# The second feed-forward product of two layers, computed as seven block products instead of eight

## The reference, cut to what matters

```python
def swiglu(h, w_gu, w_down):
    gu = jnp.einsum('bsd,df->bsf', h, w_gu)
    g, up = gu[..., :D_FF], gu[..., D_FF:]          # D_FF = 2816
    return jnp.einsum('bsf,fd->bsd', jax.nn.silu(g) * up, w_down)

# second_block, in each of two layers:
h = layer_norm(ALPHA * h + mix, ln1_g[l], ln1_b[l])
h = layer_norm(ALPHA * h + swiglu(h, w_gu[l], w_down[l]), ln2_g[l], ln2_b[l])
```

## Time and profile before

| | before |
|---|---|
| median of 3 runs | 1973.95 us (1970.31 to 1974.38) |
| span of the profiled execution, first to last instruction | 1972.4 us |
| mean granted TensorE clock | 0.971 of full speed |
| TensorE matmuls busy | 1825.4 us, 93% of the span, 10396 matmuls |
| VectorE, ScalarE, GpSimd busy | 978.2, 760.7 and 407.5 us |
| down phase of layer 0 | 1244.8 to 1364.5 us |
| down phase of layer 1 | 1840.6 to 1960.3 us |

### The profile page before, as it was taken

The page is one execution under the profiler, slowest core; times in us unless marked ns, Lnnn a source line. Parts: engine busy times, 40 slices in busy tenths (PEclk is TensorE's granted clock), DMA queues, the critical chain, the costliest instruction groups (busy, mean ns, idle before and its releaser), DMA issues.

```text
span 1972.4 us, 26603 instructions
## 1 busy us (share of the span) xinstructions
PE 1825.4 (93%) x10396; PEld 1443.2 (73%) x10396; DVE 978.2 (50%) x1919; ACT 760.7 (39%) x1392; POOL 407.5 (21%) x450
## 2 busy tenths in 40 slices
PE   7999999996998764998999999999998999999997
PEld 6888777785554434776888888888776788888886
...
PEclk9999999996999996998999999999998999999999
DMA  4344300576999993221233333232211233332321
GB/s 161 86 114 129 97 2 2 168 294 235 382 387 402 392 346 119 74 65 44 87 96 106 97 96 97 97 98 81 76 60 48 76 106 98 100 100 88 106 97 53
DMA packets 134884, 264.42 MB, mean 134 GB/s; under 512 B 11617, under 2 KB 92129, under 8 KB 122465
## 3 DMA queue, kind: packets, MB, share of 16 engines
q1 hardware_dynamic: 116752, 229.92, 33.9%
...
q0 software_dynamic: 5120, 8.40, 1.3%
...
## 4 chain that ended last, share of the span: by engine, by line
PE 54%; DMA 10%; DVE 8%; issue 2%; ACT 1%; POOL 1%; PEld 1%; PEldq 0%; POOLq 0%; ACTq 0%; DVEq 0%; SPq 0%
PE b L507 15%; PE b L509 15%; PE b L508 15%; DMA m<-in_w_gate_up 6%; PE b L2054 3%; PE b L2607 2%; DMA m<-in_w_down 1%; DVE m L2782 1%; PE b L2079 1%; PE b L2589 1%; PE b L2575 1%; DMA m<-in_w_in 1%; DVE m L715 1%; DMA s_h<-m 1%; DVE m L657 1%
## 5 line engine op out<-in xcount | busy, mean ns | idle before, releaser
L507 PE MATMUL b<-m,m 128*128 128x512 f32 (+3 forms) x2060 | 777.2, 377 | 9.8 <-DVE m L2536 4.6
L508 PE MATMUL b<-m,m 128*128 128x512 f32 (+3 forms) x2060 | 768.9, 373 | 0.0
L509 PE MATMUL b<-m,m 128*128 128x512 f32 (+3 forms) x2060 | 768.6, 373 | 0.0
L493 DVE TENSOR_TENSOR m<-m,m 128x1024 fp32r<-128x1024 f32 (+1 forms) x212 | 278.6, 1320 | 480.3 <-ACT m L483 479.6
L507 PEld LDWEIGHTS b<-m,m 128*128 128x128 f32 x2060 | 390.2, 189 | 83.9 <-issue 6.0
L509 PEld LDWEIGHTS b<-m,m 128*128 128x128 f32 x2060 | 390.0, 189 | 66.2
L508 PEld LDWEIGHTS b<-m,m 128*128 128x128 f32 x2060 | 390.4, 189 | 63.9
L483 ACT ACTIVATE m<-m 128x1024 fp32r<-128x1024 f32 (+1 forms) x236 | 245.9, 1047 | 469.7 <-PE b L509 441.0
L3037 POOL TENSOR_TENSOR m<-m,m 128x512 fp32r<-128x512 f32 x44 | 71.2, 1641 | 417.3 <-ACT m L2983 417.3
L2054 PE MATMUL b<-m,m 128*64 128x256 f32 x1024 | 126.3, 389 | 26.4 <-DMA m<-in_w_gate_up 24.8
L2054 PEld LDWEIGHTS b<-m,m 128*64 128x64 f32 x1024 | 73.4, 139 | 77.5 <-issue 38.3
...
## 6 DMA issues: line engine op xcount, KB each, us to landing
...
m<-in_w_gu SPq DMA_DIRECT2D x88, 512.0 KB, 4.3
...
m<-in_w_in SPq DMA_DIRECT2D x48, 512.0 KB, 3.9
m<-in_w_down SPq DMA_DIRECT2D x44, 512.0 KB, 3.7
...
m<-in_w_o SPq DMA_DIRECT2D x16, 512.0 KB, 3.9
...
```

The costliest lines, as they stand in the source:

```text
L493: e.tensor_tensor(flat(wlo[HX[i]], i), flat(raw[RX[i][0]], i), fr(flat(whi[HX[i]], i)), ALU.subtract).then_inc(sem("w_lo"), 1)
L507: e.matmul(out, xh, yh, start=start, stop=False, skip_group_check=True)
L508: e.matmul(out, xh, yl, start=False, stop=False, skip_group_check=True)
L509: return e.matmul(out, xl, yh, start=False, stop=stop, skip_group_check=True)
```

## The change

**The arithmetic.** Call the feed-forward activations A (tokens x features) and the weight B (features x columns), each cut in 2 x 2 blocks: A's blocks are 256 tokens by 1408 features (11 tiles), B's are 1408 features by 512 columns. Eight block products become seven (`q` = 0 to 6), each of them 11 (feature tiles) x 2 (token tiles) x 3 (passes) = 66 matmuls of 128x512, 462 in a layer. The blocks of A that enter are, for q = 0 to 6: A12, A11, SA = A21 - A22, SA - A11, A12 + SA - A11, A11 - A21 and A22. The blocks of B are B21, B11, B11 + B12, B11 + B12 + B22, B22, B12 + B22, and B11 + B12 + B22 + B21. Products are added to or subtracted from the four result blocks; `DOWN_BANKS` gives each its two PSUM banks, and q = 3 and 5 go on in the banks of the product before.

**Weight sums by DMA.** A product's weights are 6 chunks: five of 2 x 128 features and one of 1 x 128. SyncE loads the chunks of q = 0, 4 and 5 into raw cells. It loads those of q = 1 with 11 DMAs of 256 KB into a held area (`WH`, `WT`; rows of 2 x 256), when `w_used` of the last gate/up chunk is there. GpSimd then issues DMAs that add a quadrant of `w_down` to what is held (`accum_op=ADD`): 11 of 256 KB each for q = 2, 3 and 6, each after the `lo` of the same chunk of the product before was made; and 6 of 512 KB (the last 256 KB) onto the raw cells of q = 5. These 39 are one queue and are issued in this order: q = 2, 3, 6, 5. `hi_to` and `lo_to` wait for the sums (`source_in`).

**Activations.** VectorE writes the products of SiLU and up as plain float32 tiles `FR` (22 x 512). ScalarE and GpSimd make `hi` and `lo` of A11 and A12 during the eleven steps; GpSimd also makes SA and three other sums (4 operations of 128x256 for each of 11 pairs of tiles). The other five blocks get their halves in the down phase, in three parts each (`DOWN_PARTS`) between the weight chunks: ScalarE the `hi`, VectorE the `lo`, into two buffer pairs `DA` that alternate from product to product.

**Sums and layer norm.** VectorE adds results to `Hs` behind each product (`down_sums`), at chunk 2 of the next one: 18 operations of 128x512 for products 0 to 6 instead of 8. The last three chunks of q = 6 go token tile by token tile (tiles 2 and 3, 15 matmuls each), and TensorE waits for the halves of all three before the first of them. The layer norm of tiles 0 and 1 is done during products 5 and 6. The load of gain and offset (`gD`, `bD`) moves from the start of `scalar_ffn` to product 2, since SA now has that place.

The core of the diff:

```diff
+DN_FIRST = ((1, 0), (0, 0), (0, 1), (1, 1), (1, 1), (0, 1), (1, 0))
+DN_KIND = ("raw", "held", "sum", "sum", "raw", "pair", "sum")
+DN_SECOND = {2: (0, 1), 3: (1, 1), 5: (1, 1), 6: (1, 0)}
...
-        add(f"dn{l}", io["w_down_2"][l], 22, 2, (0, 512), 512)
-    return chunks, at, twins
+        wd = io["w_down_2"][l].rearrange("(k p) n -> p k n", p=P)
+        at[f"dn{l}"] = len(chunks)
+        for q, (kq, fq) in enumerate(DN_FIRST):
+            for c in range(6):
+                k, n = 11 * kq + 2 * c, min(2, 11 - 2 * c)
+                kinds[len(chunks)] = DN_KIND[q]
+                if q in DN_SECOND:
+                    k2, f2 = DN_SECOND[q]
+                    added[len(chunks)] = wd[:, 11 * k2 + 2 * c:11 * k2 + 2 * c + n, 512 * f2:512 * f2 + 512]
+                chunks.append((wd[:, k:k + n, 512 * fq:512 * fq + 512], n, 512))
...
+                if cells is None:
+                    l, c = (0 if i < CH["dn1"] else 1), down_at(i)[1]
+                    e.wait_ge(*at("w_used", CH[f"dn{l}"]))
+                    if c >= 4:
+                        e.wait_ge(*at("ff_u", 22 * l + 22))
+                    for kk in range(chunks[i][1]):
+                        e.dma_start(held_rows(c, kk), halves_of(chunks[i][0], kk)).then_inc(sem(f"w_held{c}"), 16)
...
-                e.activation(flat(whi[HX[i]], i), flat(raw[cell], i), ACT.Copy).then_inc(sem("w_hi"), 1)
+                if i == CH["mix1"]:
+                    e.wait_ge(*at("w_lo", halved_by(i - 1)))
+                e.activation(split(whi[HX[i]], i), source(i), ACT.Copy).then_inc(sem("w_hi"), 1)
...
+        DOWN_BANKS = ((6, 7), (4, 5), (2, 3), (4, 5), (0, 1), (4, 5), (6, 7))
+        DOWN_TURN = (2, 3, 4, 5)
+        DOWN_PARTS = ((0, 4), (4, 8), (8, 11))
...
+            def one(q, k, kk, x, hi, lo):
+                ah, al = DA[q % 2]
+                sl = slice(x * P, x * P + P)
+                return mm3(e, bank[swapped(l, DOWN_BANKS[q])[x]][:, :], ah[:, k, sl], al[:, k, sl], hi[:, kk, :], lo[:, kk, :],
+                           k == 0 and q not in (3, 5), k == 10 and q not in (1, 3))
...
+            for q in range(7):
+                if q == 0:
                     e.wait_ge(*at("ff_u", 22 * l + 20))
-                    e.wait_ge(*at("ff_l", 22 * l + 2))
-            def after_down(e, u):
-                if u < 10:
-                    e.wait_ge(*at("ff_l", 22 * l + 2 * u + 4))
-            behind, amid = turns(e, 2, B47) if l == 0 else (no_wait, no_wait)
-            gemm_tok(e, f"dn{l}", CH[f"dn{l}"], FAh, FAl, 22, 512, [swapped(l, B47), swapped(l, B03)], free_down, after_down, tail=3, behind=behind)
+                elif q in (2, 4):
+                    e.wait_ge(*at("ff_u", 22 * l + 22))
+                elif q in (3, 5, 6):
+                    e.wait_ge(*at(f"res_dn{l}", {3: 4, 5: 10, 6: 2}[q]))
+                for c in range(6):
+                    if q == 0:
+                        e.wait_ge(*at("ff_l", 22 * l + min(13 + 2 * c, 22)))
+                    elif q >= 2 and c % 2 == 0:
+                        e.wait_ge(*at("da_lo", 15 * l + 3 * (q - 2) + c // 2 + 1))
...
+                    if q == 6 and c >= 3:
+                        continue
+                    hi, lo = chunk(e, c0 + 6 * q + c)
+                    for kk in range(chunks[c0 + 6 * q + c][1]):
+                        for x in range(2):
+                            m = one(q, 2 * c + kk, kk, x, hi, lo)
+                    m.then_inc(sem("w_used"), 1)
...
+            w = [chunk(e, c0 + 36 + c) for c in (3, 4, 5)]
+            for x in range(2):
+                for c in (3, 4, 5):
+                    hi, lo = w[c - 3]
+                    for kk in range(chunks[c0 + 36 + c][1]):
+                        m = one(6, 2 * c + kk, kk, x, hi, lo)
+                    if x == 1:
+                        m.then_inc(sem("w_used"), 1)
+                if x == 0:
+                    m.then_inc(sem(f"mm_dn{l}"), 1)
...
+                if 1 <= q <= 5 and c >= 3:
+                    k0, k1 = DOWN_PARTS[c - 3]
+                    e.wait_ge(*at("da_s", 44 * l + 44))
+                    e.wait_ge(*at("w_used", c0 + 6 * q))
+                    e.activation(DA[(q + 1) % 2][0][:, k0:k1, :], down_block(q + 1)[:, k0:k1, :], ACT.Copy).then_inc(sem("da_hi"), 1)
+                if (q, c) == (2, 2):
+                    e.wait_ge(*at("da_lo", 15 * l + 3))
+                    e.dma_start(gD, io["ln2_g_2"][l:l + 1, :].rearrange("a n -> (a n)").partition_broadcast(P)).then_inc(sem("gD"), 16)
...
-                    e.tensor_tensor(UP[f], bank[o + 2 + f][:, :], SL[f], ALU.mult).then_inc(sem("ff_u"), 1)
+                    e.tensor_tensor(FR[:, 2 * i + f, :], bank[o + 2 + f][:, :], SL[f], ALU.mult).then_inc(sem("ff_u"), 1)
...
+        def vector_down(e, l):
+            c0, u = CH[f"dn{l}"], 2 + 2 * l
+            for p in range(42):
+                q, c = divmod(p, 6)
+                lo_to(e, c0 + p + 1)
+                if 1 <= q <= 5 and c >= 3:
+                    k0, k1 = DOWN_PARTS[c - 3]
+                    ah, al = DA[(q + 1) % 2]
+                    e.wait_ge(*at("da_hi", 15 * l + 3 * (q - 1) + c - 2))
+                    e.tensor_tensor(al[:, k0:k1, :], down_block(q + 1)[:, k0:k1, :], fr(ah[:, k0:k1, :]), ALU.subtract).then_inc(sem("da_lo"), 1)
+                if c == 2 and q >= 1:
+                    down_sums(e, l, q - 1)
+                if (q, c) == (5, 4):
+                    ln_shift(e, u, 0)
+                    ln_shift(e, u, 1)
+                elif (q, c) == (6, 4):
+                    if l == 0:
+                        gained_hi(e, 2, 0, NHhi)
+                        gained_lo(e, 2, 0, NHhi, NHlo)
+                    else:
+                        e.wait_ge(*at("gD", 64))
+                        for t in (0, 1):
+                            ln_gain(e, 4, t, gD)
+                            ln_offset_dve(e, 4, t, bD)
             if l == 0:
-                vector_layer_norm(e, 2, last, NHhi, NHlo, CH["mix1"] + 2, B47)
...
+        def gpsimd_ffn(e, l):
+            for k in range(22):
+                j = k % 11
+                if k >= 11:
+                    c = Chain(e, *at("da_s", 44 * l + 4 * j))
+                    a11, a21, a12, a22 = FR[:, j, 0:256], FR[:, j, 256:512], FR[:, k, 0:256], FR[:, k, 256:512]
+                    e.wait_ge(*at("ff_u", 22 * l + k + 1))
+                    c.inc(e.tensor_tensor(SA[:, j, :], a21, a22, ALU.subtract))
+                    c.wait()
+                    c.inc(e.tensor_tensor(a21, a11, a21, ALU.subtract))
+                    c.wait()
+                    c.inc(e.tensor_tensor(a11, SA[:, j, :], a11, ALU.subtract))
+                e.wait_ge(*at("ff_h", 22 * l + k + 1))
+                if k == 11:
+                    e.wait_ge(*at("ln_ov", 8 * l + 8))
+                ah, al = DA[k < 11]
+                e.tensor_tensor(al[:, j, :], FR[:, k, 0:256], fr(ah[:, j, :]), ALU.subtract).then_inc(sem("ff_l"), 1)
+                if k >= 11:
+                    e.wait_ge(*at("ff_l", 22 * l + k + 1))
+                    c.wait()
+                    c.inc(e.tensor_tensor(a12, a12, a11, ALU.add))
+            gpsimd_down(e, l)
+            meet(e)
+        def gpsimd_down(e, l):
+            c0, u = CH[f"dn{l}"], 2 + 2 * l
+            for q, before in ((2, 1), (3, 2), (6, 3)):
+                for c in range(6):
+                    e.wait_ge(*at("w_lo", halved_by(c0 + 6 * before + c)))
+                    for kk in range(chunks[c0 + 6 * q + c][1]):
+                        e.dma_start(held_rows(c, kk), halves_of(ADDED[c0 + 6 * q + c], kk), accum_op=ALU.add).then_inc(sem(f"w_sum{c}"), 16)
+            for c in range(6):
+                cell, of, n_landed = RX[c0 + 30 + c]
+                e.wait_ge(*at(f"w_raw{of}", n_landed))
+                e.dma_start(view(raw[cell], c0 + 30 + c), ADDED[c0 + 30 + c], accum_op=ALU.add).then_inc(sem(f"w_sum{c}"), 16)
```

More of the change, by code:

```diff
@@ L390, in build_program @@
         LAY = M.pos
+        M.pos = LAY - 8192
+        WH = [M.f(8, 512) for _ in range(2)]
+        assert M.pos == LAY
         st3 = small[:, 0:16]
@@ L591, in feat_halves @@
                         amid(0)
+                    elif half == 0 and f == 0 and k % 4 == 3:
+                        amid(1 + k // 4)
             m.then_inc(sem("w_used"), 2)
```

259 lines of the change are left out of this document (194 added, 65 removed).

## The result

The changed kernel takes **1984.8 us** (median of 4 runs, 1981.2 to 1986.6) against 1974.2 in the runs beside it (1970.3 to 1974.5): ratio 1.0055, interval 1.004 to 1.0069. It is slower by 10.6 us, where the forecast said 1962.5; the number lies in the range, beside the first rival's 1988.5. The experiments will show that the rival's mechanism was only partly the cause.

What follows compares the result with a forecast made beforehand. TensorE's matmul count was taken to bound the kernel: -29.9 + 1.4 (VectorE) + 9 (product 6's end) - 0.9 (tail) + 8 (product 5's sums) + 1 (clock) = -11.4 us, so 1962.5 us; range 1951 to 2008.

Steps and rivals of the forecast that it cites:

- the first rival: Down phases: sums at 164 GB/s or less fall behind the products, 17 us of waits a layer, 1988.5 us; chance 0.33.
- the 1.4 us for VectorE: Down phases: VectorE late where four sums stand together, behind q = 2 and 5; 0.7 us a layer, +1.4.
- the rival with VectorE as the bound: Down-phase products: DMA issues on GpSimd slow VectorE, 2006 us, or operations a tenth longer, 1965 us; chance 0.10.
- the rival of cheap sums: Down phases: sums cost what plain loads cost, so the 8 us go; -18, 1956 us; chance 0.15.
- the 8 us: Product 5 in both layers: four chunks late by 1 us each, 4 us a layer, +8.
- The end of product 6: TensorE waits for the last three chunks' halves, VectorE later still: +6 in layer 1, +3 in layer 0.
- -0.9: End of the kernel: from TensorE's end to the last output 11.2 us instead of 12.1.
- the fragile one: q = 5: load, issue, transfer, completion and splits take 11.7 us, leaving 0.9 us of slack if engines are free.
- the dense row's half: Rate of accumulating DMAs: half of the 396 GB/s of dense loads, 198 GB/s, just above the demand of 192.
- the clock: Last 30 matmuls after a 6 us wait: some at the lower clock level, +1, ends 0 and 4.
- the turns: Turns into the next layer keep their length, ends -1 and +2.
- near 180 GB/s: Sum rate, between 164 and 198, at which the first rival decides, from a wait of 9.7 us a layer.

Runs made afterwards that it cites:

- own_place_gains_last: Changed kernel with product 5's chunks in FR cells, loaded and summed earlier, layer 1's tile 0 and 1 gains after the last split, gain/offset load in product 5: 1956.2 us.

## Why the prediction was wrong

**Right.** 132 matmuls fewer at 0.2267 us. Products 1 to 4 run in 14.96 us, so VectorE, ScalarE, and GpSimd's gate and up work are hidden; the 1.4 us for VectorE weren't needed, and the rival with VectorE as the bound falls (splits of 1.21 to 1.23 us beside the DMA issues). So does the rival of cheap sums, by 166 against 335 GB/s; its own time should have read 1954.5, since taking the 8 us away from -11.4 gives -19.4 and not -18. The end of product 6: 2.1 and 6.8 us, 8.9 for a forecast of 9, on VectorE as said. From the last matmul's start to the span's end 11.45 instead of 12.5 us: -1.05 for -0.9. Product 5 was named as the fragile one, and it is where most of the time went.

**Wrong, first step: the price of the DMAs.** Between the ends 164 and 198 GB/s I chose the dense row's half; measured are 166. By the nearer row (105 GB/s at a share of 0.32) I had the other end in hand. The engines' share is 1.12 to 1.21 in products 1 to 3, where 0.8 or 0.9 was forecast. The Trainium skill, page Collectives: The Full Stack, section on the bandwidth ceiling, gives about half a copy's rate for a reduce; here it is 166 to 335 GB/s, and by that rule, the trace agrees.

**Wrong, second step, and the larger one: how the price reaches TensorE.** "Four chunks late by 1 us each: 4 us a layer" was 8.9 and 9.4. It took the chain of product 5 with latencies of an idle machine: load 3.7, sum 0.95 + 2.65 + 2.1, splits 2.3, 11.7 us in all. Measured for chunk 0 are 7.2 + 9.2 + 2.5 = 18.9 against 12.6 to be had; the forecast called this the slack "if the engines are free", then added bytes over the layer instead of stretching the chain's own steps. The first rival's time was right within 4 us, in good part by luck: it had 17 us of waits a layer where 8.9 and 9.4 were measured, and the clock and the turns below, which it didn't have, made up for a good half of that. Its mechanism is there, but small. The queue does fall behind: in layer 0 the first sum lands in 4.6 us and the last one of product 6 in 12.5, in the middle of product 4 (1314.5). But products 2 and 3 were never late, moving product 5's sums forward gave nothing, and removing product 6's gave 5 us. Nor does it decide whether 11 sums fit into one product, the rival's "near 180 GB/s": with the sums of products 2, 3 and 6 at a plain load's price 14.3 of 18.3 us of waits stay, and own_place_gains_last beats the old kernel at the same 2.0 times price.

**Wrong, third: the clock.** +1 was forecast. Behind the three long waits (6.3, 7.0 and 6.8 us) TensorE's steps are 0.43 us for 8 to 14 matmuls; what they have above 0.2267 is 1.9, 1.7 and 2.8 us: **+6.4**. No such stretch was there before.

**Wrong, fourth: the turns**, put at nothing, with ends -1 and +2. From the start of the last 128x512 matmul of layer 0's down phase to the next mixer's landmark it takes 20.1 us (1366.66 to 1386.75) instead of 16.6 (1366.79 to 1383.38): **+3.5**. TensorE's turns wait 3.1 instead of 1.25 us there, and the clock was 0.76 (1376 to 1383) instead of full. (The phase of layer 0 before really ended at 1367.0: the 1364.5 of the table above is its start plus 528 steps, and turns stand among its last matmuls.)

Together, for the two stages: -29.9 + 18.3 (product 5) + 8.9 (product 6) + 6.4 (clock) + 3.5 (turns) - 1.05 (tail) = +6.2, measured +7.9. The wait of 0.4 at the start of product 6 in layer 1 makes part of the 1.7 left, and each wait is counted from the end of a record, 0.16 us after the next step was due, five times; the last 0.5 isn't attributed.
